# Selected-keys attention by groups of three heads with queries split ahead, and one output tile begun in the last stick-breaking pair

## The reference, cut to what matters

```python
def one_block(args):                       # 128 queries; 8 such blocks
    ...
    _, sel = lax.top_k(score, topk)        # 256 keys chosen by an indexer
    logits = jnp.einsum('bqgrd,bqkgd->bqgrk', qg, k_sel) * att_scale
    logits = jnp.where(valid[:, :, None, None, :], logits, -jnp.inf)
    p = jax.nn.softmax(logits, axis=-1)
    o = jnp.einsum('bqgrk,bqkgd->bqgrd', p, v_sel)
y_att = dsa_attention(q, k, v, qi, ki, wi) @ w_att_out[l]   # 6 heads of 64, 2 key groups

# second block, stick breaking: 12 heads of 64, strictly causal
w = jnp.where(strict, jnp.exp(jax.nn.log_sigmoid(z) + later), 0.0)
outs.append(jnp.einsum('bhts,bhsd->bhtd', w, vb))
y = jnp.concatenate([mix, mem_out], axis=-1) @ w_out[layer]
```

## Time and profile before

| | |
|---|---|
| median of 3 runs | 3147.85 us (3146.23 to 3148.41) |
| the profiled execution's own time | 3153.3 us |
| its span in the trace | 3151.5 us |
| mean granted clock of PE | 0.96 |
| PE busy | 2962.3 us |
| DVE busy | 1690.4 us |

### The profile page before, as it was taken

One profiled execution on the slowest core, in us unless ns is written; L12 is line 12 of the kernel. 1 busy time (PEld: TensorE's weight loads), 2 busy tenths in 40 slices (PEclk: granted clock), 3 DMA queues, 4 the chain that ended last, 5 costly groups with the idle time before them and its releaser, 6 DMA issues.

```text
span 3151.5 us, 35444 instructions
## 1 busy us (share of the span) xinstructions
PE 2962.3 (94%) x13362; PEld 2385.4 (76%) x13362; DVE 1690.4 (54%) x2322; ACT 781.9 (25%) x1429; POOL 1160.1 (37%) x649
## 2 busy tenths in 40 slices
PE   7987999998999899999999889999798999999997
PEld 4675878885777688888888668887675888888885
DVE  3475899985553533232332647888937333333327
ACT  4154011103531211011110355666613000000003
POOL 2330434441023334333443415555532433344331
PEclk9978999996999999999999999999898999999998
DMA  3110112221032111111111210000020111111111
GB/s 144 41 34 7 47 67 81 80 80 67 1 130 71 41 47 47 47 53 47 47 47 49 72 67 27 27 21 27 21 87 27 47 51 49 47 47 47 53 47 61
DMA packets 45054, 165.41 MB, mean 52 GB/s; under 512 B 4880, under 2 KB 6160, under 8 KB 43920
## 3 DMA queue, kind: packets, MB, share of 16 engines
q1 hardware_dynamic: 37168, 129.31, 12.4%
q10 hardware_dynamic: 7776, 34.61, 2.8%
HBM read 147.12 MB, written 16.78 MB: 52 GB/s over the span
## 4 chain that ended last, share of the span: by engine, by line
PE 82%; DVE 12%; ACT 2%; issue 2%; DVEq 1%; DMA 0%; POOL 0%; ACTq 0%; SPq 0%; POOLq 0%
PE dense L517 21%; PE dense L518 20%; PE dense L521 20%; DVE a_lo L1543 2%; DVE stay L1935 2%; PE dense L908 2%; PE side L813 2%; PE dense L909 2%; PE dense L910 2%; PE dense L557 1%; PE dense L823 1%; PE dense L558 1%; PE dense L559 1%; PE dense L740 1%; PE side L946 1%
## 5 line engine op out<-in xcount | busy, mean ns | idle before, releaser
L426 POOL TENSOR_TENSOR w_hi<-raw,zero 128x1024 fp32r<-128x1024 f32 x210 | 400.8, 1908 | 1572.2 <-PE dense L521 1300.2
L517 PE MATMUL dense<-a_hi,w_hi 128*128 128x512 f32 x2000 | 783.4, 392 | 14.1 <-DVE T L1681 5.6
L518 PE MATMUL dense<-a_lo,w_hi 128*128 128x512 f32 x2000 | 780.4, 390 | 0.0
L521 PE MATMUL dense<-a_hi,w_lo 128*128 128x512 f32 x2000 | 617.9, 390 | 0.0
L428 POOL TENSOR_TENSOR w_lo<-raw,w_hi 128x1024 fp32r<-128x1024 f32 x210 | 526.4, 2506 | 16.5
L517 PEld LDWEIGHTS dense<-a_hi,w_hi 128*128 128x128 f32 x2000 | 376.7, 188 | 95.7 <-issue 7.7
L521 PEld LDWEIGHTS dense<-a_hi,w_lo 128*128 128x128 f32 x2000 | 376.9, 188 | 78.9
L518 PEld LDWEIGHTS dense<-a_lo,w_hi 128*128 128x128 f32 x2000 | 376.7, 188 | 79.0 <-issue 1.2
L517 PE MATMUL dense<-b_hi,w_hi 128*128 128x512 f32 x832 | 327.2, 393 | 5.2 <-DVE T L1841 2.5
L518 PE MATMUL dense<-b_lo,w_hi 128*128 128x512 f32 x832 | 324.7, 390 | 0.0
L1821 DVE TENSOR_TENSOR x_res<-x_res,dense 128x1024 f32<-128x1024 f32 x100 | 122.1, 1221 | 329.6 <-PE dense L521 328.3
(11 more groups left out here) (263 smaller groups left out, 4405.6 us busy)
## 6 DMA issues: line engine op xcount, KB each, us to landing
raw<-in_w_stream SPq DMA_DIRECT2D x231, 512.0 KB, 3.4
x_in<-in_x_t SPq DMA_DIRECT2D x8, 512.0 KB, 7.3
spill_gate<-T ACTq DMA_DIRECT2D x8, 512.0 KB, 2.6
spill_part<-gates ACTq DMA_DIRECT2D x8, 512.0 KB, 2.7
back<-spill_gate ACTq DMA_DIRECT2D x8, 512.0 KB, 3.7
back<-spill_part ACTq DMA_DIRECT2D x8, 512.0 KB, 4.7
x_res<-in_x_t ACTq DMA_DIRECT2D x2, 2048.0 KB, 9.0
spill_x<-x_res ACTq DMA_DIRECT2D x1, 4096.0 KB, 13.5
```

Source lines behind the costliest of these rows:

```text
L426: pool.tensor_tensor(w_hi[:, r % 2, :], raw[:, r, :], zero[:, 0:1].broadcast_to([P, D]), ALU.add).then_inc(weights_rounded, 1)
L517: pe.matmul(o, w_hi[:, slot, w], hi[:, k, x], start=b == 0, stop=False)
L518: pe.matmul(o, w_hi[:, slot, w], lo[:, k, x], start=False, stop=False)
L521: last = pe.matmul(o, w_lo[:, slot, w], hi[:, k, x], start=False, stop=stop)
```

## The change

**Attention.** A step is now one of 16 groups, three heads that share their keys (query block `i`, key group `g`). Each group's work is cut by blocks of 128 keys into turns, 72 in all: a turn is three transposes into one bank of PSUM, one copy of 384 columns by ACT into `att_probs_t`, and one product with the values of 384 columns, three turns later. The logits are made from split operands: keys as `kk_hi` and `kk_lo` with the same 64 rows twice, one below the other, and queries `qq` with the high part on one half of the partitions and the low part on the other, so that two fp32r matmuls of 128 partitions (L865, L866) take the place of one float32 matmul of 64. Keys are split ahead of the convolution's loop, the queries of the first four groups behind it, the others one by one at the turns of `QUERIES_AT`. The probabilities lie in nine strips; the logits of nine heads are made ahead and of the others at the turns of `LOGITS_AT`. The sign is turned, so that the row's minimum serves as bias without the multiplication of L1730. The mask is made for one query block at a time. The meetings around the loop are gone, ACT loads its table for the exponential ahead of it, the load of `m_in` stands behind the loop, and the first half of the T_ATT product starts when four of eight blocks of `ya` are done.

**The last pair.** `EARLY_AT` begins three steps earlier (127, 129, ... 139). Four of its seven low parts are made by POOL (L527), the other three by DVE. At `FIRST_AT` (steps 130, 132, ... 142) PE makes one block each of the tile T_OUT2+1. Behind the pair come seven blocks of T_OUT2, and then the eighth block of both.

```diff
-DSA_PLAN = [(i, h) for i in range(TB) for h in range(ATT_H)]
+DSA_PLAN = [(i, g) for i in range(TB) for g in range(GROUPS)]
...
+DSA_LEAD, DSA_LAG, DSA_STRIPS, DSA_QUERIES = 3, 2, 9, 4
+def logits_at(s, j):
+    first, last = DSA_X0[s - 2] - 1, DSA_X0[s - 1] - 2
+    return first + (last - first) * j // (REP - 1)
...
-EARLY_AT = {PAIR_STEPS * (SB_H // 2 - 1) + 10 + 2 * j: j for j in range(EARLY)}
+EARLY_AT = {PAIR_STEPS * (SB_H // 2 - 1) + 7 + 2 * j: j for j in range(EARLY)}
+FIRST_AT = {n + 3: j for n, j in EARLY_AT.items()}
...
                         split_part(T_SB + t, part)
+                    if n in EARLY_AT and EARLY_AT[n] % 2 == 0:
+                        j, k = EARLY_AT[n], Y2_ORDER[EARLY_AT[n]]
+                        pool.wait_ge(parts["y2"][0], j + 1)
+                        pool.tensor_tensor(a_lo[:, k, :], y2_f[:, k, :], a_hi[:, k, :].bitcast(F32), ALU.subtract
+                                           ).then_inc(y2_low, 1)
...
-                        last = pe.matmul(side[:, n % 2, c:e], q_f[r, h % 3, i * P:i * P + P], k_f[r, c:e], start=True,
-                                         stop=True)
...
+                    pe.matmul(side[:, n % 2, c:e], qq[:, s % DSA_QUERIES, j, :], kk_hi[g][:, c:e], start=True, stop=False)
+                    last = pe.matmul(side[:, n % 2, c:e], qq[:, s % DSA_QUERIES, j, :], kk_lo[g][:, c:e], start=False, stop=True)
...
+            for n in range(REP * DSA_LEAD):
+                att_logits(n)
+            for x in range(len(DSA_TURNS) + DSA_LAG):
+                if x < len(DSA_TURNS):
+                    att_turn(x)
+                for n in LOGITS_AT.get(x, ()):
+                    att_logits(n)
+                if x >= DSA_LAG:
+                    att_values(x - DSA_LAG)
+
+            pe.wait_ge(weights_split, T_ATT + 1)
+            pe.wait_ge(parts["ya"][1], TB // 2)
+            half_product(T_ATT, dense[:, T_ATT % 2, cols(0)], ya_hi, ya_lo, 0, 0, 3, 3)
...
+                if n in FIRST_AT:
+                    j = FIRST_AT[n]
+                    if j == 0:
+                        pe.wait_ge(v_split, SB_H)
+                        pe.wait_ge(weights_split, T_OUT2 + 2)
+                    pe.wait_ge(parts["y2"][1] if j % 2 else y2_low, j // 2 + 1)
+                    product((T_OUT2 + 1) % 2, halves(dense, (U_OUT2 + 1) % 2), a_hi, a_lo, j + 1, begin=j, end=False, order=Y2_ORDER)
...
+            product(T_OUT2 % 2, halves(dense, U_OUT2 % 2), a_hi, a_lo, EARLY, end=False, order=Y2_ORDER)
+            pe.wait_ge(parts["y2"][1], KB // 2)
...
-            sc = score[:, score_at(2):score_at(TB)]
-            dve.tensor_scalar(sc, sc, TAKEN / 2, NEG, ALU.is_gt, ALU.mult)
-            meet(dve, "dve", met_n)
...
+            def normalise(n):
+                e = n % 8
+                dve.wait_ge(d_exp, n + 1)
+                dve.reciprocal(inv_sum[:, e:e + 1], row_sum[:, e:e + 1])
+                dve.drain()
+                dve.tensor_scalar(strip_of(n), strip_of(n), inv_sum[:, e:e + 1], None, ALU.mult).then_inc(d_probs, 1)
...
+            for x in range(len(DSA_TURNS)):
+                if x in QUERIES_AT:
+                    split_queries(QUERIES_AT[x])
+                for n in LOGITS_AT.get(x, ()):
+                    mask(n)
+                for n in LOGITS_AT.get(x - 1, ()):
+                    normalise(n)
```

More of the change, by code:

```diff
@@ new lines, in att_turn, with att_values @@
+            def att_turn(x):
+                s, kb = DSA_TURNS[x]
+                if kb == 0:
+                    pe.wait_ge(d_probs, REP * (s + 1))
+                if x >= 2:
+                    pe.wait_ge(d_copied, x - 1)
+                for j in range(REP):
+                    last = pe.transpose(att_turn_bank(x)[:, j * P:j * P + P],
+                                        strip_of(REP * s + j)[:, kb * P:kb * P + P], ident[:, :])
+                last.then_inc(d_turned, 1)
+            def att_values(x):
+                s, kb = DSA_TURNS[x]
+                if kb == 0 and s >= 2:
+                    pe.wait_ge(d_taken, s - 1)
+                pe.wait_ge(d_copied, x + 1)
+                pe.matmul(att_out_bank(s), v_f[:, kb, :], pt[:, x % 4, :], start=kb == 0, stop=kb == DSA_PLAN[s][0]
+                          ).then_inc(d_out, 1)
@@ L1154, in _, with round_queries @@
             meet(act, "act", met_n)
+            def round_queries(s):
+                i, g = DSA_PLAN[s]
+                if s >= DSA_QUERIES:
+                    act.wait_ge(d_ready, REP * (s - DSA_QUERIES + 1))
+                act.activation(qq[group_rows(g), s % DSA_QUERIES, :, :], q_f[group_rows(g), :, i * P:i * P + P], ACT.Copy,
+                               scale=-SCALE).then_inc(q_high, 1)
+            for g in range(GROUPS):
+                for half in (g, 1 - g):
+                    last = act.activation(kk_hi[g][group_rows(half), :], k_f[group_rows(g), :], ACT.Copy)
+                last.then_inc(k_round, 1)
             for j in range(3):
@@ L1164, in _ @@
                 act.activation(yc_hi[:, j, :], T[:, 2, :], ACT.Copy).then_inc(parts["yc"][0], 1)
+            act.wait_ge(parts["yc"][1], 3)
+            for s in range(DSA_QUERIES):
+                round_queries(s)
             def gate_blocks(i):
@@ L1195, in _ @@
                 act.wait_ge(part_spilled[j], 64)
-            meet(act, "act", met_n)
-            def fetch(j):
-                act.dma_start(back[:, 2 * (j % 2), :], spill_gate[j]).then_inc(fetched[j % 2], 16)
-                act.dma_start(back[:, 2 * (j % 2) + 1, :], spill_part[j]).then_inc(fetched[j % 2], 16)
[L1203 to L1221, removed]
@@ L1694, in _ @@
                 low((yc_hi[:, j, :], yc_lo[:, j, :]), j, T[:, 2, :], "yc", j + 1)
+            for s in range(DSA_QUERIES):
+                split_queries(s)
             def gate_blocks(i):
@@ L1952, in _ @@
                     k = Y2_ORDER[j]
-                    low((a_hi[:, k, :], a_lo[:, k, :]), k, y2_f[:, k, :], "y2", j + 1)
+                    if j % 2:
+                        low((a_hi[:, k, :], a_lo[:, k, :]), k, y2_f[:, k, :], "y2", j + 1)
             for j in range(EARLY, KB):
```

169 lines of the change are left out of this document (119 added, 50 removed).

## The result

The changed kernel takes 3119.14 us (median of 4 runs, 3118.72 to 3120.0), the kernel before 3148.13 in the same series (4 runs): a ratio of 0.9908, 95% interval 0.9896 to 0.9920. It is faster by 29 us. The prediction was 3095 with a range of 3075 to 3118, so the direction was right and the time lies outside the range, 1.1 us beyond its slow end.

The account below looks back on a forecast made before the run. PE was taken to bound the kernel on the whole, busy for 2962 of 3151.5 us. From 3147.85 us, attention at -55 and the last pair at +2.3 gave 3095, with an 8-in-10 range of 3075 to 3118.

Parts of the forecast that it names:

- The start: Attention's start: without the meeting behind the gates, `side` is free at 727.10 us and the first turn starts at about 735.
- The splits around the convolution at nothing: Key and query splits around the convolution: some 7.1 us on DVE, covered by 7.3 us of waits for PE, cost nothing.
- Turns 0 to 19: Attention at two to four key blocks: DVE sets the pace, 34.4 us, so turn 20 comes at about 773.5.
- Turns 20 to 71: Attention's later turns, bound by PE: 52.5 us of turns, 15.7 of logits, 8 of waits at groups' first turns.
- The tail: Attention's end: half a us to the T_ATT product, at 850.3; its first half no longer waits, 2.0 us more gained.
- ACT's order binds: Rival in attention: exponentials waiting for DVE hold up ACT's copies, waits 1.8 us not 0.8; +10, 3105 us; chance 0.12.
- The clock: Attention: TensorE's granted clock was assumed to rise early in turns 0 to 19; the sum needs 1.00 in later turns.
- the rival that kept it low to four key blocks: Rival in attention: the clock stays low up to four or five key blocks; +20, 3115 us; chance 0.15.
- The serial one: Rival in attention: turns run as a serial chain; +99, 3249 us; slower above 2.3 us a turn; chance 0.03.
- the small stall: Rival in the last pair: the port binds less, POOL's low parts are shorter; 7 us better, 3088 us; chance 0.20.
- The pair: Last stick-breaking pair: stall +7.4, later steps +3.0, blocks taken out -9.5, wait ahead of T_OUT2+2 +2.9, clock -1.5; sum +2.3 us.
- The port: Last pair: DVE and POOL share SBUF ports, so POOL's low parts relieve DVE of nothing; side by side, 7 us lower.

Follow-up runs that it names:

- e5: Changed kernel with both ACT's exponentials and DVE's query split issued one turn later: 3091.51 us, ratio 0.9823 to the kernel before.
- e3: Changed kernel with ACT's exponentials issued one turn later: 3094.76 us, ratio 0.9829 to the kernel before.
- e4: Changed kernel with DVE's split of the queries one turn later: 3096.81 us, ratio 0.9835 to the kernel before.
- e2: The last pair's part of the change alone, put into the kernel before: 3154.7 us against 3150.63 in its series, ratio 1.0018.
- e7: Changed kernel with all seven low parts of the last pair made by DVE, none by POOL: 3116.87 us, ratio 0.9904 to the kernel before.
- e6: Changed kernel with the first two blocks of T_OUT2+1 made together at step 132: 3114.42 us, ratio 0.9896 to the kernel before.

## Why the prediction was wrong, by its own steps

**The start: right.** The first logits came at 727.43 and the first turn at 734.75, against 727.1 and about 735.

**The splits around the convolution at nothing: right.** PE's last gate product started at 725.20 us against 725.13 before.

**Turns 0 to 19: the step failed, by 8.2 us.** The text had DVE set the pace, busy nearly throughout, and turn 20 at 773.5. It came at 781.69, with DVE busy for only two thirds. What was missing is the wait for ACT's rounding, 10.5 us in this stretch, of which the prediction knew nothing: it counted the query split's 0.6 us of work, and not that on DVE it stands ahead of the masks and waits for an engine whose queue waits for masks. In e5, without the ring, turn 20 came at 771.99, near the forecast, but not by DVE's pace: DVE was busy for 30.65 of 37 us, PE for 34.02 at a granted clock of 0.88. That this time was met is partly luck, for the sum had its counts wrong too: up to turn 20 `LOGITS_AT` and `QUERIES_AT` hold 22 masks and 8 splits, not 19 and five, and the prices were too high.

**Turns 20 to 71: the step failed, by about 7.6 us.** "In about eight places a group's first turn waits on its last head ... 8 us." The turn itself was sized right: three transposes and the product with the values come at a pitch of 0.975 us (1.01 forecast), the product taking 0.65 (0.66). But the 51 pitches from turn 20 to turn 71 took 83.8 us, where 76.2 were given for 52, and that with the logits of 17 heads left, not 20. ACT's waits for masks were not eight but 33 in the stage, and PE's gaps for the copy 14 with 17.7 us. So the waits did not come at groups' first turns alone. PE was also slower at its work: busy for 69.4 us here where e5 has 64.5, at a mean granted clock of 0.96 and not 1.00.

**The tail: 4 us more.** From the last turn's transposes to the place that stands for the first T_ATT product (872.38 - 4.08 = 868.3, the first `side` product less 18 matmuls of 0.227) it took 2.8 us; the forecast had half a us and gave 2.0 back. One of the forecast's 52 pitches lies in it, for three products with the values still stand behind the last transposes. (A product follows its turn by two turns, `DSA_LAG`, and not by three as the part on the change has it.) Together with the terms above this makes the 20.0 between 868.3 and 848.3, so the attention gave -34.9 in place of -55. About 1.7 us more came in the merge behind it: the first addition to `x_res` is at 919.57 against 956.14, 36.6 earlier.

**The rival that came true** is "ACT's order binds", with a chance of 0.12 and a price of 10 us. e3 and e4 show it to be the cause, and its price to be some 27 us (e5). What made the estimate small was that I priced one wait along one queue, at eight places. It was a ring over two queues, and a delay in it comes back a turn later.

**The clock: right on its rise, not on the rest.** The granted clock was 0.50 from 735 to 745 us and 0.92 from there to 760, so it rose early, and the rival that kept it low to four key blocks did not happen. The sum's condition, 1.00 in turns 20 to 71, was not met: it was 0.96.

**The other rivals.** The serial one did not come: three transposes and a product have a pitch of 0.975 us, and from the first turn to the last a turn took 1.84 us on average with all that belongs to it, below the 2.3 at which the sign turns. Nor did the small stall. Its premise, a low part of 1.1 us on DVE, misreads the trace before, where the six in the window took 1.21 to 1.89.

**The pair: the sum was near, +2.9 by the traces and +4 by e2's medians against +2.3, by terms that partly cancelled.** The stall of step 131 was 7.2 (7.4): the split's end came at 2218.71 (forecast 2256.0, less the 37.1 that the pair then was earlier, 2218.9). The block behind it took 2.70 us, not 1.36, at a granted clock of 0.50, but then the small product on DVE took 0.16, not 1.2. The steps to 143 cost 0.8, not 3.0: POOL's low parts took 2.4 each as forecast, but the granted clock there went from 0.78 to 1.00, and DVE was busy for 28.96 of 31.1 us in place of all of them. The wait ahead of T_OUT2+2 was 3.2 us (2.9; its own rows give 3.0). With the 9.5 taken out as forecast these make 1.7; the other 1.2 of the 2.9 lie in none of my terms. "From below the stall is 2.1 less, if POOL's low part fits into POOL's idle time" is what e7 decides: counted from the scan of step 120 the split ended 29.6 us later before, 32.0 in the change and 31.6 in e7. So POOL's low part cost the split 0.4 us, not 2.5. The other 2.0 are there in e7 too, so they came by the steps themselves, which now hold the work of `EARLY_AT` three steps earlier. That the sum met the stall's end was luck in this term.

**The port.** e7 bears out that a low part on POOL is no relief for DVE: with all on DVE the pair is 1.6 us shorter up to the first product behind it, by the trace alone. The times cannot tell it. But that it relieves DVE "of nothing" is a little too strong. One of POOL's low parts in the change, and DVE beside it:

```profile
2244.78 2.40 POOL L527 TENSOR_TENSOR a_lo<-y_f,a_hi 128x1024 fp32r<-128x1024 f32 x1
2244.83 0.68 DVE L2064 TENSOR_TENSOR y_f<-dense,out_low 64x512 f32<-64x512 f32 x1 [0.50 <-ACT out_low L1481]
...
2245.94 1.25 DVE L2074 TENSOR_TENSOR stick_weights<-stick_weights,stay 128x1 f32<-128x1 f32 x1 [0.43 <-ACT stay L1494]
```

The operation on one column, both of whose inputs lie in SBUF, takes 1.25 us and ends with POOL's at 2247.18; alone it takes 0.16 (2223.43). The addition with one input in PSUM (`dense`) lies wholly beside POOL's and takes 0.68 us, as it does with POOL idle (0.68, at 2265.74).

## What to carry to other kernels

Where two in-order engines feed each other in one turn of a pipeline, write down for each instruction that waits what stands behind it in its queue, and follow that around: if the path comes back to the first engine, the turn costs the sum of the ring, whatever the engines' busy times say. Its sign here was that DVE, ACT and PE were all busy for only 66 to 78% of the first stretch. The cure cost one line: put the consumer one turn later in its queue, where the producer has long been done. Here one turn was enough, and one place of the ring gave nearly all of it.

A product that is put into a stage bound by another engine, to fill PE's gaps, must not stand ahead of the work that this engine waits for, if the product has to wait itself. e6 moved it by two steps and the stall of 7.0 us was gone, though half of it came back in the steps behind.

## What the runs showed that I had not expected

Two edits worth 25 and 23 us alone gave 27 together. The granted clock went with the gaps: in the change PE waited 2.02, 2.42 and 3.16 us ahead of transposes at 770, 787 and 829 us, and the windows of 20 us around them showed 0.91; in e3, whose waits there are 1.35 us at most, they showed 1.00. It is no strict rule: the window from 800 us, with a wait of 2.61, showed 1.00. In the change one block of six matmuls, with PE idle for 8.76 us before it, took 2.70 us (2218.81 to 2221.51), while such a block takes 1.36 in a steady stretch.
